# Writing the head sums of the attention output: four copies by ScalarE and one add in SBUF, in place of two copies and two adds out of PSUM

## The chip, the core and the metric

The kernel runs on one core of one Trainium2 chip. The metric is the device time of one execution in microseconds (us). The kernel before took 1492.64 us (median of 3 runs, 1490.17 to 1496.86). Engines are named as the profile names them: PE is TensorE (PEld its weight loads), ACT is ScalarE, DVE is VectorE, POOL is GpSimd, SP is the engine that issues the DMAs.

## The reference

One decoder layer over 1024 tokens of width 1024: stick-breaking attention with 16 heads of 64, a 4-head cross-attention into 256 memory tokens, one output projection, and a SwiGLU feed-forward part. What the change touches is the end of the stick-breaking attention, the product with the values:

```python
z = jnp.einsum('bhqd,bhkd->bhqk', qi, k).astype(jnp.float32) * SCALE
past = kpos[None, :] < tpos[:, None]
log_fail = jnp.where(past, jax.nn.log_sigmoid(-z), 0.0)
after = lax.cumsum(log_fail, axis=3, reverse=True) - log_fail
a = jnp.where(past, jnp.exp(jax.nn.log_sigmoid(z) + after), 0.0)
return jnp.einsum('bhqk,bhkd->bhqd', a.astype(v.dtype), v)
```

## The kernel before

Every matrix product is made in full precision out of rounded parts: each operand is split into a high part (fp32r, copied by ACT) and a low part (what is left, subtracted by DVE), and PE adds the products of the parts up in PSUM.

The attention runs over 8 head pairs, s = 0 to 7 (PAIRS). Pairs 0 to 5 run in a loop, so that addresses and semaphore counts there come out of registers; pairs 6 and 7 are written out. A pair has 12 units (UNITS: one query tile of 128 rows against up to 512 keys), and the units make four groups of two query tiles, which end at units 1, 3, 7 and 11 (GROUP_END). For a unit PE computes scores (line 310), ACT takes two sigmoids of them (fail, line 391, and succ, line 397), DVE scans fail (lines 478 and 483) and multiplies (line 491), PE transposes the product (line 320), ACT and DVE split the transposed weights (a_h, line 405, and a_l, line 504), and every second unit PE multiplies them with the values into o_ps, one bank of PSUM (line 336). Between these PE does filler: in pairs 0 to 6 the next pair's input projection (pe_part, line 282), in the last pair the output projection (pe_project, line 882). Each engine runs its own instructions strictly in the order written out in pe_step, act_step and dve_step, and the engines meet at semaphores.

The value product puts the high and the low half of v side by side as 128 stationary columns, so that o_ps holds, for head h, two halves of 64 partitions and 256 columns that must still be added: for h = 0 the heads' rows are 0 to 63 and the low part is in rows 64 to 127; for h = 1 it is the other way about. act_low_rows (lines 408 to 414) copies the two low quarters into pv_low, on the partitions of their heads. dve_heads (lines 507 to 517) then adds, in two instructions of 64 partitions, the high quarter out of PSUM and pv_low, into o_t (om_t for pairs 6 and 7). Semaphore s_pl counts the copies (low_part_copied), s_o the adds (heads_written). PE opens a new group in o_ps (start=True) only when s_o says that the group before has been added (line 331), and ACT overwrites pv_low only then (line 412).

For the groups ending at units 1, 3 and 7 both helpers are called one unit later, inside the pair: act_low_rows between act_high and act_fail, dve_heads after dve_weights. The group ending at unit 11 is handled at the pair's end: ACT does act_v (v_s high, line 384), then act_low_rows, then the next pair's act_fail for unit 2. DVE does it in dve_open (lines 519 to 526) of the next pair: two scans, dve_heads, dve_weights (line 491), dve_v (line 468). PE's first transposes of the next pair (line 320) wait for that dve_v, because they go to the same banks. In the last pair ACT and DVE also split the attention output and w_out for the output projection (lines 730 and 736), and POOL makes the low parts of w_out (line 736). The cross-attention has helpers of its own (lines 845 to 858), which the change leaves as they are.

Of the kernel before, what the change touches and what calls it, by code (L numbers as in the profile page):

```python
# [5 lines left out]
ALU = mybir.AluOpType  # L6
ACT = mybir.ActivationFunctionType
# [5 lines left out]
P = 128  # L13
BANK = 512
HD = 64
# [4 lines left out]
def trunk(nc, x, mem, attn_norm, mem_norm, w_mem_kv, xq_norm, xk_norm, w_out, ffn_norm, w_gate, w_up, w_down,  # L20
          sb_w_in, out):
    _, S, D = x.shape
# [3 lines left out]
    PAIRS = D // (2 * HD)  # L26
# [29 lines left out]
    with ExitStack() as ctx:  # L56
        cursor = [-(-nc.sbuf_base // 32) * 32]
        
        def at(name, shape, dt, off):
            return nc.alloc_sbuf_tensor_at(name, shape, dt, offset=off)  # L60
# [7 lines left out]
        def take(name, shape, dt=F32, columns=None):  # L68
            t = at(name, [shape[0], columns] if columns else shape, dt, cursor[0])
            cursor[0] += size(shape)  # L70
            return t

        def sem(name):
            return ctx.enter_context(nc.semaphore(name))
# [24 lines left out]
        o_t = take("o_t", [P, PAIRS * S])  # L99
# [25 lines left out]
        pv_low = take("pv_low", [P, 2 * P])  # L125
# [23 lines left out]
        om_t = at("om_t", [P, 2 * S], F32, mk_at)  # L149
# [29 lines left out]
        t_ps, j_ps, z_ps, o_ps = ps[:, 0:2], ps[:, 2:4], ps[:, 4:7], ps[:, 7]  # L179
# [26 lines left out]
        s_pl = sem("low_part_copied")  # L206
        s_o = sem("heads_written")
# [115 lines left out]
        def pe_values(pe, s, u, par):  # L323

            i, k0, w, _ = UNITS[u]
            w_first = UNITS[u - 1][2]
            opens = UNITS[u][3]
            pe.wait_ge(s_tl, 1 + TUSE * s + u + 1)
            if opens:
                g = (i - 1) // 2  # L330
                pe.wait_ge(s_o, 8 * s + 2 * g + 1)
            for h in range(2):
                for j in range(w // P):
                    q0 = 0 if j * P < w_first else P
                    for t, a in enumerate((a_h, a_l)):
                        mm = pe.matmul(o_ps[:, h * 2 * P + q0:(h + 1) * 2 * P],  # L336
                                       v_s[par][:, k0 // P + j, 2 * h:2 * h + 2, :].rearrange("p a d -> p (a d)"),
                                       a[:, h, j, q0:2 * P],
                                       start=(opens and h == 0 and j == 0 and t == 0), stop=False,
                                       skip_group_check=True)  # L340
            mm.then_inc(s_pv, 1)
# [66 lines left out]
        def act_low_rows(act, s, u):  # L408

            g = UNITS[u][0] // 2  # L410
            act.wait_ge(s_pv, 1 + NU // 2 * s + u // 2 + 1)
            act.wait_ge(s_o, 8 * s + 2 * g + 1)
            act.activation(pv_low[0:HD, :], o_ps[HD:P, 0:2 * P], ACT.Copy).then_inc(s_pl, 1)
            act.activation(pv_low[HD:P, :], o_ps[0:HD, 2 * P:4 * P], ACT.Copy).then_inc(s_pl, 1)

        def act_step(act, s, par, last=False):
            side = iter(SPLITS) if last else None
# [26 lines left out]
            if not last:  # L444
                act_v(act, 1 - par, 1 + TUSE * s + NU)
            act_low_rows(act, s, NU - 1)


# [57 lines left out]

        def dve_heads(dve, s, u):
            g = UNITS[u][0] // 2
            dve.wait_ge(s_pl, 8 * s + 2 * g + 2)
            for h in range(2):  # L510
                r = slice(HD * h, HD * h + HD)
                if isinstance(s, int) and s >= PAIRS - 2:
                    dst = om_t[r, (s - PAIRS + 2) * S + g * 2 * P:(s - PAIRS + 2) * S + (g + 1) * 2 * P]
                else:
                    dst = o_t[r, bass.ds(s * S + g * 2 * P, 2 * P)]
                dve.tensor_tensor(dst, o_ps[r, h * 2 * P:(h + 1) * 2 * P],
                                  pv_low[r, :], ALU.add).then_inc(s_o, 1)

        def dve_open(dve, s, par):

            dve_scan(dve, s, 1, 0)
            dve_scan(dve, s, 1, 1)
            if not (isinstance(s, int) and s == 0):
                dve_heads(dve, s - 1, NU - 1)
            dve_weights(dve, s, 1)
            dve_v(dve, par, TUSE * s)
# [129 lines left out]
        def turn_ps(g):  # L656

            return ps[:, (0, 1, 4, 5)[g % 4]] if g < XU0 else t_ps[:, g % 2]
# [46 lines left out]
        def operand(i):  # L705

            what, k, half = i
            if what == "w":
                return wo_raw[:, W_ORDER.index(i) % 4], wo_h[:, k], wo_l[:, k]
            c = slice(half * BANK, (half + 1) * BANK)  # L710
            if k in (PAIRS - 2, PAIRS - 1):
                src = om_t[:, (k - PAIRS + 2) * S + half * BANK:(k - PAIRS + 2) * S + (half + 1) * BANK]
            else:
                at_ = (k if k < PAIRS else k - 2) * S + half * BANK
                src = o_t[:, at_:at_ + BANK]
            return src, o_h[k][:, c], o_l[k][:, c]

        def act_split(act, i):
            what, k, half = i
            src, high, _ = operand(i)  # L720
            if i == SPLITS[0]:
                act.wait_ge(s_pj, W1)
            if what == "o" and k >= PAIRS - 2 and k < PAIRS:
                act.wait_ge(s_o, 8 * (k + 1) + 1)
            if what == "w":
                N = W_ORDER.index(i)
                act.wait_ge(s_wo[N % 4], 16 * (N // 4 + 1))
                if half:
                    act.wait_ge(s_op, NT if k < EARLY else 2 * NT)
            act.activation(high, src, ACT.Copy).then_inc(s_sh, 1)  # L730
# [7 lines left out]
        def wait_split(eng, i):  # L738

            e, n = LOW[i]  # L740
            eng.wait_ge(s_sl[e], n)
# [368 lines left out]
        def _(sp):  # L1110
# [27 lines left out]
            for N in range(2 * OC):  # L1138
                if N == 2:
                    sp.wait_ge(s_pj, W1 - 2)  # L1140
                if N == OC + 4:

                    sp.wait_ge(s_o, 8 * PAIRS + 1)
                    for t in range(NT):
                        sp.dma_start(x2[:, t, 0:BANK], xd[:, t, 0:BANK]).then_inc(s_x2l[0][t], 16)
                if N >= 4:
                    wait_split(sp, W_ORDER[N - 4])
                _, k, n = W_ORDER[N]
                sp.dma_start(wo_raw[:, N % 4], wod[:, k, n * BANK:(n + 1) * BANK]).then_inc(s_wo[N % 4], 16)
# [43 lines left out]
        def _(act):  # L1193
# [6 lines left out]
            for g in range(4):  # L1200
                act.wait_ge(s_xt, g + 1)
                for i in range(2):
                    last = act.activation(m_hh[:, 2 * g + i], turn_ps(g)[:, i * M:(i + 1) * M], ACT.Copy,
                                          scale=gains[:, 1, 2 * g + i:2 * g + i + 1])
                last.then_inc(s_xh, 1)
            for k in range(4):
                act_mem_w(act, k)
# [60 lines left out]
            for i in LATER + SECOND:  # L1268
                act_split(act, i)
# [265 lines left out]
```

## Time and profile before

| | |
|---|---|
| median of the runs | 1492.64 us |
| lowest and highest run | 1490.17, 1496.86 us |
| profiled execution | 1497.44 us, of which its span 1495.5 us |
| mean granted clock of TensorE | 0.976 |
| start, projections and cross-attention | 0 to 164 us |
| attention over 8 head pairs, with its last products | 164 to 683 us |
| output projection, feed-forward part | 683 to 1495 us |

The page's first part gives the busy time of each engine. Waits are told as "waiting engine and line <- releasing engine and line". A timeline row gives the start, the duration, engine, line and operation, and in brackets how long the engine had sat idle and who ended that. Instructions of an engine overlap by a little, so the distance between two starts, and not the duration, is what an instruction costs its queue.

### The profile page before, as it was taken

How to read it: one execution, taken by the hardware profiler on the slowest of the kernel's cores; microseconds unless marked ns; L12 is line 12 of the kernel's file. 1: busy time of each engine (PE TensorE's matmuls, PEld its weight loads, DVE VectorE, ACT ScalarE, POOL GpSimd, SP SyncE). 2: the span in 40 equal slices, each digit the busy share in tenths (PEclk: the TensorE clock that was granted, in tenths of full speed). 3: DMA queues.
4: the chain of work that ended last, by engine and by line, in shares of the span. 5: the costliest groups of instructions: out<-in, count | busy, mean ns of one | idle time of the engine just before them, and what ended most of it. 6: DMA issues, size and time to landing. Idle time of an engine off the chain costs nothing.

```text
span 1495.5 us, 19957 instructions
## 1 busy us (share of the span) xinstructions
PE 1433.4 (96%) x7212; PEld 1173.9 (79%) x7212; DVE 864.2 (58%) x1292; ACT 558.9 (37%) x947; POOL 30.0 (2%) x31
## 2 busy tenths in 40 slices
PE   6998899999999999699999999999999999999998
PEld 4776687787877878588887888888888888888887
DVE  5446798898988989795253353342525334252535
ACT  6444566565565655562242212121211212121110
POOL 0000000000000000213000000000000000000000
PEclk8997999999999999699999999999999999999999
DMA  6100100010000100104111211110211111021102
GB/s 211 43 14 15 29 22 22 24 33 28 21 21 22 35 27 30 40 18 149 35 57 39 72 60 40 45 56 28 70 42 56 42 42 56 28 71 43 57 14 113
DMA packets 92610, 69.91 MB, mean 47 GB/s; under 512 B 7312, under 2 KB 78992, under 8 KB 92560
## 3 DMA queue, kind: packets, MB, share of 16 engines
q1 hardware_dynamic: 92560, 69.24, 15.0%
q8 instruction: 32, 0.52, 0.2%
q14 instruction: 18, 0.15, 0.0%
HBM read 65.03 MB, written 4.19 MB: 46 GB/s over the span
## 4 chain that ended last, share of the span: by engine, by line
PE 89%; DVE 5%; ACT 2%; issue 2%; SPq 1%; DMA 0%; DVEq 0%; ACTq 0%
PE ps L989 32%; PE ps L1040 16%; PE ps L282 15%; PE ps L882 7%; PE ps L336 5%; PE ps L320 5%; PE ps L310 3%; PE ps L253 2%; PE ps L700 1%; PE ps L233 1%; PE ps L839 1%; DVE hl L682 1%; DVE succ L491 1%; DVE v_s L468 1%; PE ps L671 1%
## 5 line engine op out<-in xcount | busy, mean ns | idle before, releaser
L989 PE MATMUL ps<-f_h,gw_h 128*128 128x512 f32 x704 | 275.2, 391 | 1.9 <-DVE f_l L682 1.9
L989 PE MATMUL ps<-f_l,gw_h 128*128 128x512 f32 x704 | 274.6, 390 | 0.0
L989 PE MATMUL ps<-f_h,gw_l 128*128 128x512 f32 x704 | 274.5, 390 | 0.0
L1056 DVE TENSOR_TENSOR x<-ps,x 128x512 f32<-128x512 f32 x176 | 121.5, 691 | 80.7 <-PE ps L1040 77.5
L989 PEld LDWEIGHTS ps<-f_h,gw_h 128*128 128x128 f32 x704 | 132.5, 188 | 29.4 <-issue 2.1
L989 PEld LDWEIGHTS ps<-f_h,gw_l 128*128 128x128 f32 x704 | 132.6, 188 | 27.7
L989 PEld LDWEIGHTS ps<-f_l,gw_h 128*128 128x128 f32 x704 | 132.6, 188 | 27.4
L405 ACT ACTIVATE a_h<-ps 128x256 fp32r<-128x256 f32 (+2 forms) x96 | 78.0, 813 | 169.5 <-PE ps L320 169.4
L282 PE MATMUL ps<-hh,w_h 128*128 128x512 f32 x336 | 140.7, 419 | 0.0
L1040 PE MATMUL ps<-dw_h,gu_h 128*128 128x512 f32 x352 | 136.9, 389 | 0.0
L1040 PE MATMUL ps<-dw_l,gu_h 128*128 128x512 f32 x352 | 136.9, 389 | 0.0
L1040 PE MATMUL ps<-dw_h,gu_l 128*128 128x512 f32 x352 | 136.9, 389 | 0.0
L282 PE MATMUL ps<-hh,w_l 128*128 128x512 f32 x336 | 132.7, 395 | 0.0
L282 PE MATMUL ps<-hl,w_h 128*128 128x512 f32 x336 | 132.4, 394 | 0.0
L1014 DVE TENSOR_TENSOR prod<-ps,sig 128x512 f32<-128x512 f32 x44 | 30.4, 692 | 146.6 <-PE ps L989 133.4
L504 DVE TENSOR_TENSOR a_l<-ps,a_h 128x256 fp32r<-128x256 f32 (+2 forms) x96 | 91.6, 954 | 39.4 <-ACT a_h L405 38.6
L1021 ACT ACTIVATE gu_h<-prod 128x512 fp32r<-128x512 f32 x44 | 27.8, 632 | 213.6 <-DVE prod L1014 213.6
L478 DVE TENSOR_TENSOR_SCAN fail<-fail,own 128x129 f32<-128x129 f32 (+3 forms) x128 | 102.5, 828 | 1.5 <-ACT fail L391 1.3
L320 PE MATMUL ps<-ident,succ 128*128 128x128 f32 x576 | 83.0, 281 | 18.7 <-DVE a_l L504 8.1
L491 DVE TENSOR_TENSOR succ<-fail,succ 128x256 f32<-128x256 f32 (+2 forms) x96 | 93.6, 975 | 0.3
L966 ACT ACTIVATE gw_h<-f_raw 128x512 fp32r<-128x512 f32 x88 | 53.0, 625 | 104.1 <-DMA f_raw<-in_w_up 101.9
L320 PEld LDWEIGHTS ps<-ident,succ 128*128 128x128 f32 x576 | 65.4, 143 | 31.3 <-issue 10.4
(172 smaller groups left out, 2369.4 us busy)
## 6 DMA issues: line engine op xcount, KB each, us to landing
w_raw<-in_sb_w_in SPq DMA_DIRECT2D x52, 256.0 KB, 2.9
f_raw<-in_w_gate SPq DMA_DIRECT2D x44, 256.0 KB, 3.0
f_raw<-in_w_up SPq DMA_DIRECT2D x44, 256.0 KB, 2.9
f_raw<-in_w_down SPq DMA_DIRECT2D x44, 256.0 KB, 2.7
wo_raw<-in_w_out SPq DMA_DIRECT2D x20, 256.0 KB, 2.7
x_in<-in_x SPq DMA_DIRECT2D x8, 512.0 KB, 8.4
x<-in_x SPq DMA_DIRECT2D x16, 256.0 KB, 6.1
out<-x SPq DMA_DIRECT2D x8, 512.0 KB, 2.6
```

What stands on the lines that cost most here:

```text
L282: mm = pe.matmul(j_ps[:, 0], w[:, kc // 4, kc % 4], h[:, kc, half * BANK:(half + 1) * BANK], start=(kc == 0 and i == 0), stop=(kc == KC - ...
L320: mm = pe.transpose(t_ps[:, h, j * P:(j + 1) * P], succ[:, u % 2, h, j * P:(j + 1) * P], ident[:, :])
L336: mm = pe.matmul(o_ps[:, h * 2 * P + q0:(h + 1) * 2 * P], v_s[par][:, k0 // P + j, 2 * h:2 * h + 2, :].rearrange("p a d -> p (a d)"), a[:, ...
L405: act.activation(a_h[:, :, 0:w // P, col * P:(col + 1) * P], t_ps[:, :, 0:w].rearrange("p h (j q) -> p h j q", q=P), ACT.Copy).then_inc(s_ ...
L478: dve.tensor_tensor_scan(back, back, own[:, BANK - w:BANK + 1][:, ::-1], 0.0, ALU.mult, ALU.max).then_inc(s_scan, 1)
L491: done = dve.tensor_tensor(g, f[:, :, 1:w + 1], g, ALU.mult)
L504: dve.tensor_tensor(a_l[:, :, 0:w // P, c], t_ps[:, :, 0:w].rearrange("p h (j q) -> p h j q", q=P), a_h[:, :, 0:w // P, c].bitcast(F32), A ...
L882: mm = pe.matmul(out_bank(i), o[k][:, t * P:(t + 1) * P], w[:, k], start=(at_ == 0 and j == 0), stop=(at_ == len(order) - 1 and j == 2))
L966: act.activation(ffn_w(kind, par, j, True), (f_raw2 if extra_slot(r) else f_raw)[:, j % 2], ACT.Copy).then_inc(s_fh, 1)
L989: mm = pe.matmul(ps[:, 4 + 2 * fb + mat], w[:, fb, mat, k], f[half][:, k], start=(k == 0 and i == 0), stop=(k == KC - 1 and i == 2))
L1040: mm = pe.matmul(ps[:, (2, 3, 0, 1)[d % 4]], g[par][:, fb, t * P:(t + 1) * P], w[:, fb, n * BANK:(n + 1) * BANK], start=(fb == 0 and i == ...
L1056: dve.tensor_tensor(o, ps[:, (2, 3, 0, 1)[d % 4]], o, ALU.add).then_inc(s_x2, 1)
```

## The change

ACT now copies all four quarters out of o_ps: for each h first the low quarter into pv_low, then the high quarter straight into o_t (or om_t) at its place, given by a new helper heads_at. DVE adds pv_low to o_t in place, in SBUF, as one instruction over 128 partitions. So ACT has four copies for each group where it had two, and DVE one add where it had two. s_pl counts four for each group, s_o one. PE opens the next group when s_pl says that all four copies are made, no longer when DVE has added. DVE waits for all four copies; ACT still waits for the previous group's add before it overwrites pv_low. A count of one is added to s_pl at the kernel's start, by a copy of the memory tokens' part, as s_o has one from DVE, and the counts on s_o elsewhere (act_split, the SP queue) are adapted.

```diff
--- before.py
+++ after.py
@@ -328,7 +328,7 @@
             pe.wait_ge(s_tl, 1 + TUSE * s + u + 1)
             if opens:
                 g = (i - 1) // 2
-                pe.wait_ge(s_o, 8 * s + 2 * g + 1)
+                pe.wait_ge(s_pl, 16 * s + 4 * g + 1)
             for h in range(2):
                 for j in range(w // P):
                     q0 = 0 if j * P < w_first else P
@@ -409,9 +409,19 @@
 
             g = UNITS[u][0] // 2
             act.wait_ge(s_pv, 1 + NU // 2 * s + u // 2 + 1)
-            act.wait_ge(s_o, 8 * s + 2 * g + 1)
-            act.activation(pv_low[0:HD, :], o_ps[HD:P, 0:2 * P], ACT.Copy).then_inc(s_pl, 1)
-            act.activation(pv_low[HD:P, :], o_ps[0:HD, 2 * P:4 * P], ACT.Copy).then_inc(s_pl, 1)
+            act.wait_ge(s_o, 4 * s + g + 1)
+            for h in range(2):
+                r, other = slice(HD * h, HD * h + HD), slice(HD - HD * h, P - HD * h)
+                cols = slice(h * 2 * P, (h + 1) * 2 * P)
+                act.activation(pv_low[r, :], o_ps[other, cols], ACT.Copy).then_inc(s_pl, 1)
+                act.activation(heads_at(s, g, r), o_ps[r, cols], ACT.Copy).then_inc(s_pl, 1)
+
+        def heads_at(s, g, r):
+
+            if isinstance(s, int) and s >= PAIRS - 2:
+                at_ = (s - PAIRS + 2) * S + g * 2 * P
+                return om_t[r, at_:at_ + 2 * P]
+            return o_t[r, bass.ds(s * S + g * 2 * P, 2 * P)]
 
         def act_step(act, s, par, last=False):
             side = iter(SPLITS) if last else None
@@ -506,15 +516,9 @@
 
         def dve_heads(dve, s, u):
             g = UNITS[u][0] // 2
-            dve.wait_ge(s_pl, 8 * s + 2 * g + 2)
-            for h in range(2):
-                r = slice(HD * h, HD * h + HD)
-                if isinstance(s, int) and s >= PAIRS - 2:
-                    dst = om_t[r, (s - PAIRS + 2) * S + g * 2 * P:(s - PAIRS + 2) * S + (g + 1) * 2 * P]
-                else:
-                    dst = o_t[r, bass.ds(s * S + g * 2 * P, 2 * P)]
-                dve.tensor_tensor(dst, o_ps[r, h * 2 * P:(h + 1) * 2 * P],
-                                  pv_low[r, :], ALU.add).then_inc(s_o, 1)
+            dve.wait_ge(s_pl, 16 * s + 4 * g + 5)
+            both = heads_at(s, g, slice(0, P))
+            dve.tensor_tensor(both, both, pv_low[:, :], ALU.add).then_inc(s_o, 1)
 
         def dve_open(dve, s, par):
 
@@ -721,7 +725,7 @@
             if i == SPLITS[0]:
                 act.wait_ge(s_pj, W1)
             if what == "o" and k >= PAIRS - 2 and k < PAIRS:
-                act.wait_ge(s_o, 8 * (k + 1) + 1)
+                act.wait_ge(s_o, 4 * (k + 1) + 1)
             if what == "w":
                 N = W_ORDER.index(i)
                 act.wait_ge(s_wo[N % 4], 16 * (N // 4 + 1))
@@ -1140,7 +1144,7 @@
                     sp.wait_ge(s_pj, W1 - 2)
                 if N == OC + 4:
 
-                    sp.wait_ge(s_o, 8 * PAIRS + 1)
+                    sp.wait_ge(s_o, 4 * PAIRS + 1)
                     for t in range(NT):
                         sp.dma_start(x2[:, t, 0:BANK], xd[:, t, 0:BANK]).then_inc(s_x2l[0][t], 16)
                 if N >= 4:
@@ -1202,6 +1206,8 @@
                 for i in range(2):
                     last = act.activation(m_hh[:, 2 * g + i], turn_ps(g)[:, i * M:(i + 1) * M], ACT.Copy,
                                           scale=gains[:, 1, 2 * g + i:2 * g + i + 1])
+                    if g == 0 and i == 0:
+                        last.then_inc(s_pl, 1)
                 last.then_inc(s_xh, 1)
             for k in range(4):
                 act_mem_w(act, k)
```

## Rows read from the trace of the kernel before

**Rows 1.** the page: busy time, share of the span and instructions of each engine

```profile
PE 1433.4 (96%) x7212; PEld 1173.9 (79%) x7212; DVE 864.2 (58%) x1292; ACT 558.9 (37%) x947; POOL 30.0 (2%) x31
```

**Rows 2.** busy time of stretches of the attention, columns PE to POOL, granted clock, DMA

```profile
295.00:360.00 65.00, 62.49 (x384) 51.05 (x382) 56.12 (x74) 37.81 (x59) 0.00 (x0) 1.00 0.08 24
555.00:620.00 65.00, 56.33 (x347) 46.95 (x347) 53.38 (x70) 36.53 (x56) 2.75 (x2) 0.90 0.10 33
620.00:683.00 63.00, 56.16 (x313) 46.62 (x312) 54.45 (x63) 39.70 (x64) 11.39 (x8) 0.91 0.11 34
```

**Rows 3.** waits of 164 to 683 us: waiting engine, releaser, total, times, longest

```profile
DVE o_t L516 <- ACT pv_low L414: 22.3, 6, 3.7
PE ps L320 <- DVE a_l L504: 8.1, 8, 1.0
PE ps L320 <- DVE v_s L468: 6.7, 7, 3.5
```

**Rows 4.** instructions of line 516: duration ns min/median/max, first and last start

```profile
L516 DVEq FUSED_REGOPS  x48: 57/57/57, 180.0 to 543.7; - x48
L516 DVE TENSOR_TENSOR o_t<-ps,pv_low x48: 405/422/429, 181.7 to 544.1; 64x256 f32 x48
```

**Rows 5.** the first of the two copies into pv_low, same columns

```profile
L413 ACT ACTIVATE pv_low<-ps x32: 381/382/385, 179.2 to 680.4; 64x256 f32<-64x256 f32 x32
```

**Rows 6.** ScalarE in order of time, one pair's end: start, duration, instruction

```profile
291.85 1.03 ACT L384 ACTIVATE v_s<-ps 128x1024 fp32r<-128x1024 f32 x1 [2.16 <-PE ps L293]
292.90 0.38 ACT L413 ACTIVATE pv_low<-ps 64x256 f32<-64x256 f32 x1
293.31 0.38 ACT L414 ACTIVATE pv_low<-ps 64x256 f32<-64x256 f32 x1
293.71 0.81 ACT L391 ACTIVATE fail<-ps 128x768 f32<-128x768 f32 x1
```

**Rows 7.** VectorE in order of time, same stretch

```profile
288.52 0.41 DVE L491 TENSOR_TENSOR succ<-fail,succ 128x256 f32<-128x256 f32 x1
288.85 1.27 DVE L478 TENSOR_TENSOR_SCAN fail<-fail,own 128x257 f32<-128x257 f32 x2
293.83 0.88 DVE L516 TENSOR_TENSOR o_t<-ps,pv_low 64x256 f32 x2 [3.70 <-ACT pv_low L414]
294.74 0.69 DVE L491 TENSOR_TENSOR succ<-fail,succ 128x512 f32<-128x512 f32 x1
295.46 1.23 DVE L468 TENSOR_TENSOR v_s<-ps,v_s 128x1024 fp32r<-128x1024 f32 x1
```

**Rows 8.** TensorE in order of time, same stretch

```profile
296.74 0.44 PE L320 MATMUL ps<-ident,succ 128*128 128x128 f32 x2 [0.51 <-DVE v_s L468]
298.20 0.66 PE L320 MATMUL ps<-ident,succ 128*128 128x128 f32 x4 [1.02 <-DVE a_l L504]
```

**Rows 9.** ScalarE in order of time, a group inside a pair

```profile
317.80 0.60 ACT L405 ACTIVATE a_h<-ps 128x512 fp32r<-128x512 f32 x1 [1.21 <-PE ps L320]
```

**Rows 10.** all engines in order of time, last pair

```profile
632.68 0.38 ACT L414 ACTIVATE pv_low<-ps 64x256 f32<-64x256 f32 x1
634.90 0.63 ACT L730 ACTIVATE o_h<-o_t 128x512 fp32r<-128x512 f32 x1
635.57 0.69 DVE L736 TENSOR_TENSOR o_l<-o_t,o_h 128x512 fp32r<-128x512 f32 x1 [0.86 <-ACT o_h L730]
639.41 0.39 PE L336 MATMUL ps<-a_h,v_s 128*128 128x256 f32 x1 [0.65 <-DVE a_l L504]
```

**Rows 11.** GpSimd and VectorE in order of time, last pair

```profile
620.49 1.26 POOL L736 TENSOR_TENSOR wo_l<-wo_raw,wo_h 128x512 fp32r<-128x512 f32 x1 [6.16 <-ACT wo_h L730]
620.80 2.03 DVE L491 TENSOR_TENSOR succ<-fail,succ 128x1024 f32<-128x1024 f32 x1
```

**Rows 12.** busy time of shorter stretches, columns as in rows 2

```profile
116.00:120.00 4.00, 4.00 (x21) 3.42 (x20) 1.61 (x7) 0.67 (x2) 0.00 (x0) 0.61 0.01 4
355.00:360.00 5.00, 4.01 (x20) 2.56 (x16) 3.36 (x5) 2.16 (x6) 0.00 (x0) 1.00 0.00 0
```

## The prediction

> **What bounds the kernel now.** I read the page first: PE is busy for 96% of the span [rows 1]. Then the stretches: in a steady stretch of the attention PE is busy for 62.49 of 65 us, DVE for 56.12, ACT for 37.81 [rows 2]. So DVE is nearly full, but PE is fuller: all that a lighter DVE can give back in such a stretch is part of PE's 2.5 us of holes. Only where the last two pairs meet are the holes larger: 8.7 us from 555 to 620 and 6.8 us from 620 to 683, at a mean clock of 0.90 and 0.91 [rows 2].
>
> Third, the waits, to see who makes PE's holes. Seven times PE's transposes at a pair's start wait for DVE's v_s, 6.7 us in all, and eight times for a_l right behind, 8.1 us in all [rows 3]. No row of the waits has PE waiting for line 516, so the wait of pe_values that the change moves from s_o to s_pl is never late today. And DVE waits for ACT's copy at line 414: six times with 22.3 us in the loop [rows 3], that is 3.7 us at each pair's end.
>
> Fourth, the timelines of one pair's end, which put these waits into one chain. ACT copies v_s at 291.85, then the two low quarters at 292.90 and 293.31, and is past them at 293.71 [rows 6]. DVE has been idle for 3.70 us when it starts the adds at 293.83. Behind them stand the multiply of unit 1 (294.74) and the low part of v_s (295.46) [rows 7], and for that last one PE has been idle for 0.51 us when it goes on at 296.74 [rows 8]. This chain sets PE's time at seven pair ends. The second hole, 1.02 us [rows 8], is PE to ACT to DVE and back for unit 0: it keeps its length and moves with the first.
>
> **The change, part by part.** The sum is made on the profiled execution (1497.44 us, span 1495.5), as a difference, and carried to the median of 1492.64, which is 4.8 us (0.3%) lower.
>
> Two more copies of a quarter on ACT for each of 32 groups. One takes 0.382 us [rows 5]; from start to start, two cost 293.71 - 292.90 = 0.81 us [rows 6]. The new ones have the same shape and source and go to SBUF too, so I take 0.81 us for two, 26 us more for ACT in all. In the loop their destination comes out of a register, which no copy of this stage has today. Nearest is DVE's line 516, with a register operation of 57 ns for each [rows 4], and its instructions are no longer for it. I take nothing, since ACT's queue stands before instructions that are still running while it works addresses out; the other end is 57 ns and about as much again to issue it, 0.11 us for each copy, 0.23 for a group. Below nothing I exclude: nothing is taken from ACT.
>
> DVE's two adds become one. Today they hold the queue for 294.74 - 293.83 = 0.91 us [rows 7]. No add of 128 partitions by 256 columns out of SBUF into SBUF is there, but line 491 is a product of that very size, both inputs in SBUF: it takes 0.41 us and the next starts 0.33 us behind it [rows 7]. I take 0.33, a gain of 0.58 us for a group. The other end is an add as dear as the two together, a gain of zero; 0.44, if the next instruction can't overlap, lies between. Shorter than 0.33 I exclude, since the same number of columns takes that elsewhere.
>
> At a pair's end both lie in the chain. DVE waits for all four copies, so it starts 0.81 us later, and its queue is free 0.58 us sooner: the multiply, v_s and PE's transposes come 0.23 us later. Seven ends make 7 x 0.23 = 1.6 us. With the dear add it is 7 x 0.81 = 5.7 us; with the register operations on ACT 6 x 0.23 = 1.4 us come on top. Queued behind ACT's copies is the next pair's fail for unit 2, at 293.71; DVE scans it only behind v_s, which ends at 296.69 [rows 7], and the fail would be ready at 293.71 + 0.81 + 0.81 = 295.33, so this delay is covered by 1.4 us.
>
> Inside a pair three groups each put 0.81 us into ACT's queue ahead of fail, succ, a weight copy and the next a_h. ACT's idle time before that a_h is the cover: the tightest of a pair I found is 1.21 us, at 317.80 [rows 9], so 0.40 is left. If that cover were gone, a_h, a_l and then PE's value product would be late by what is missing. DVE gains 0.58 us there, but PE isn't waiting for it, so the gain becomes idle time of DVE. I cost all of this at nothing.
>
> The last pair is different, since ACT also makes the splits there and its queue is full. At unit 4 the copy at 632.68 is followed by fail, succ and the o_h of 634.90; DVE has been idle for 0.86 us when it takes the low part of that at 635.57, then scans, makes a_l, and PE has been idle for 0.65 us for it at 639.41 [rows 10]. Nothing in that chain has slack, and DVE's cheaper add lies before its own wait for o_h. So 0.81 us go to the path once. The other two groups of that pair stand before transposes that ACT waits for. Bounds: zero, if the 0.81 us are swallowed by a later wait for DVE, and 1.6 us, if a second group of that pair is as tight.
>
> Behind the last group the copies end 0.81 us later, the add some 0.2 us later, and with it SP's loads of x; PE is in projections that don't need them yet: nothing. PE's earlier leave to open a group is worth nothing, as no row has it waiting.
>
> The Trainium skill has a rule against this change ("SBUF — State Buffer", section Who interferes with whom): a DVE instruction with two SBUF inputs contends with a GpSimd instruction that reads SBUF, and one of them blocks for the whole of the other. Today's add has one input in PSUM, the new one has both in SBUF. In the last pair POOL makes wo_l at 620.49, and a DVE product that started at 620.80 took 2.03 us [rows 11], where 0.41 and 0.69 us for 256 and 512 columns [rows 7] give about 1.25 for its 1024: the trace agrees. By the rule each of the five adds that come after POOL's start could wait up to the 1.26 us of a POOL instruction, 6.3 us in all, and the sum would be 1501.4 us; today's adds would by it never wait. It is part of rival (d).
>
> Those five are the last group of pair 6 and the four of pair 7. The other 27 are free of this: POOL does nothing in the steady stretch (0.00 us) and 2.75 us from 555 to 620 [rows 2].
>
> Sum: 1.6 + 0.8 = 2.4 us, so 1492.6 + 2.4 = 1495.1 us.
>
> **The rivals.** (a) DVE's load counts after all. If DVE set the pace, a pair would gain 3 x 0.58 = 1.7 us and eight pairs 14 us: 1479 us. For it speaks DVE's 56 of 65 us [rows 2]; against it that PE's holes come from latency at a pair's start and not inside a pair, and that all holes of a steady stretch are 2.5 us. (b) The clock falls, slower than before. At a pair's end PE is busy for 4.01 of 5 us today and stays at 1.00 [rows 12], that is 2.4 GHz. The longer hole could let it fall to 1.2 GHz. The nearest price is the stretch from 116 to 120, where PE was busy throughout at a mean of 0.61 [rows 12]: 4 x 0.39 = 1.6 us of work lost. Six ends of the loop make 9.4 us: 1504.5. It decides from the point where the two holes, now 1.5 us together, lengthen enough; 0.23 us seems little, and a mean below 1.00 stands only beside holes of 7 to 9 us [rows 2]. (c) The add is as dear as the two it replaces, or the register operations stand in the path: 5.7 + 1.4 + 0.8 = 7.9 us, so 1500.5. Against it stands the product of the same size. (d) POOL and ACT's full queue in the last pair: two blocked adds and a second tight group, 2 x 1.26 + 0.8 more: 1498.4. (e) The change doesn't do what it says, for one if ACT's copies go slower side by side with PE's writes; the wait of 22.3 us [rows 3] would grow by more than 0.81 us an end. That ends like (c).
>
> **How the numbers follow.** A measurement of this kernel tells about 0.5% (7.5 us) from no change. The forecast has 0.74, (a) 0.06, (b) 0.06, (c) and (e) together 0.07, (d) 0.07. Of (a) two thirds would be over 7.5 us faster: 0.04. Slower by over 7.5 us are (b) and about half of (c) and (e): 0.10. The rest, 0.86, is within 0.5%. The range: below, the forecast without the last pair's 0.8 us and with the spread of the runs (2.5 us below the median) is 1491.8, and some 2 us for holes of the last two pairs that happen to close, 1490; above, (c) with a little of the spread, 1501.5.
>
> **What would show it.** In the changed kernel: four copies at 0.40 us from start to start; one add of about 0.41 us with the next instruction 0.33 us behind its start; DVE's idle time before it at a pair's end near 4.5 us where it was 3.70; PE's first hole of a pair near 0.75 us where it was 0.51; ACT's idle time before a_h of unit 5 near 0.4 us; DVE's busy time down by some 14 us and ACT's up by some 24 us, with a span almost unchanged. The prediction is wrong if PE's holes inside a pair shrink or grow, if the clock of a loop pair falls below 1.00, or if the add takes over 0.6 us.

## The result

The changed kernel took 1499.68 us (median of 20 runs, 1493.41 to 1501.25) against 1493.47 us for the kernel before (20 runs, 1488.17 to 1497.94). The ratio is 1.0032, with a 95% interval of 1.0021 to 1.0043: 4.8 us slower, between 3.1 and 6.4 (the medians lie 6.2 us apart, the means 5.1). That is beyond the measurement's uncertainty and within the 0.5% that the forecast counted as no change. Later runs of both kernels on another chip gave 1.0043 (1.0028 to 1.0058), 6.4 us. The forecast of 1495.1 us, 2.4 us slower, had the sign and half the size.

### The profile page after: what moved, and what is told of

Same layout as the page of the kernel before. It is cut to its first block, busy times and chain, and to the rows that moved or that the text cites. A ratio compares the mean times of both kernels' runs of the same rounds, so it can differ in the third digit from the quotient of the medians.

```text
span 1496.6 us, 20013 instructions
## 1 busy us (share of the span) xinstructions
PE 1432.8 (96%) x7212; PEld 1175.3 (79%) x7212; DVE 850.4 (57%) x1260; ACT 583.3 (39%) x1011; POOL 29.9 (2%) x31
## 4 chain that ended last, share of the span: by engine, by line
PE 88%; DVE 5%; ACT 3%; issue 2%; DMA 1%; SPq 1%; ACTq 0%; DVEq 0%
PE ps L993 31%; PE ps L1044 16%; PE ps L282 15%; PE ps L886 7%; PE ps L336 5%; PE ps L320 5%; PE ps L310 3%; PE ps L253 2%; PE ps L704 1%; PE ps L233 1%; PE ps L843 1%; DVE hl L686 1%; DVE v_s L478 1%; DMA mw_raw<-in_w_mem_kv 1%; PE ps L675 0%
```

## The profile of the changed kernel

The profiled execution took 1498.44 us, its span was 1496.6 us. Its first section, busy time and instructions of each engine, against [rows 1]:

```profile
PE 1432.8 (96%) x7212; PEld 1175.3 (79%) x7212; DVE 850.4 (57%) x1260; ACT 583.3 (39%) x1011; POOL 29.9 (2%) x31
```

DVE is 13.8 us lighter (864.2 to 850.4) and ACT 24.4 us heavier (558.9 to 583.3), as the change says. The spans differ by only 1.1 us because the start of the kernel, which the change leaves alone, happened to run 2.8 us faster in this execution; medians and stretches tell more than the two spans.

The instructions of the change, first those of o_t and pv_low (duration ns min/median/max), then ACT and DVE in order of time at one pair's end, against [rows 5], [rows 6] and [rows 7]:

```profile
L416 ACT ACTIVATE pv_low<-ps x64: 375/379/383, 176.4 to 681.9; 64x256 f32<-64x256 f32 x64
L521 DVE TENSOR_TENSOR o_t<-o_t,pv_low x24: 420/425/427, 178.9 to 542.7; 128x256 f32 x24
```

```profile
351.21 1.03 ACT L384 ACTIVATE v_s<-ps 128x1024 fp32r<-128x1024 f32 x1 [2.16 <-PE ps L293]
352.26 0.38 ACT L416 ACTIVATE pv_low<-ps 64x256 f32<-64x256 f32 x1
352.67 0.38 ACT L417 ACTIVATE o_t<-ps 64x256 f32 x1
353.07 0.38 ACT L416 ACTIVATE pv_low<-ps 64x256 f32<-64x256 f32 x1
353.47 0.38 ACT L417 ACTIVATE o_t<-ps 64x256 f32 x1
353.87 0.81 ACT L391 ACTIVATE fail<-ps 128x768 f32<-128x768 f32 x1
```

```profile
353.99 0.42 DVE L521 TENSOR_TENSOR o_t<-o_t,pv_low 128x256 f32 x1 [4.54 <-ACT o_t L417]
354.33 0.69 DVE L501 TENSOR_TENSOR succ<-fail,succ 128x512 f32<-128x512 f32 x1
354.94 1.22 DVE L478 TENSOR_TENSOR v_s<-ps,v_s 128x1024 fp32r<-128x1024 f32 x1
```

Four copies stand 0.40 us apart, the register operations of two of them cost nothing that can be seen, and ACT is past them 1.61 us after the first began, where two took 0.81. The add takes 0.42 us and the multiply starts 0.34 us behind it. New is the next distance: v_s starts 0.61 us behind the multiply, where it was 0.72 in [rows 7]. PE in order of time, against [rows 8]:

```profile
356.21 0.44 PE L320 MATMUL ps<-ident,succ 128*128 128x128 f32 x2 [0.65 <-DVE v_s L478]
357.65 0.66 PE L320 MATMUL ps<-ident,succ 128*128 128x128 f32 x4 [1.01 <-DVE a_l L514]
```

The first hole of a pair is 0.65 us here, where this pair's was 0.54 in the trace before; the second is unchanged. In the six pair ends that open pairs 1 to 6, the first hole grew from 0.51 to 0.59 us to 0.61 to 0.71 us: 0.10 to 0.12 us each.

So far this is a change of 0.1 us. What the forecast had only as an unlikely rival is in the stretches behind two of the pair ends (columns as in [rows 2]: busy time of PE, PEld, DVE, ACT and POOL, granted clock, DMA):

```profile
354.00:358.00 4.00, 2.34 (x12) 1.49 (x11) 3.58 (x6) 1.93 (x4) 0.00 (x0) 1.00 0.00 0
358.00:362.00 4.00, 4.00 (x25) 3.48 (x24) 4.00 (x6) 3.38 (x5) 0.00 (x0) 1.00 0.22 65
416.00:420.00 4.00, 2.42 (x11) 1.47 (x9) 3.18 (x6) 1.89 (x4) 0.00 (x0) 1.00 0.00 0
420.00:424.00 4.00, 3.94 (x13) 3.23 (x14) 4.00 (x6) 3.19 (x5) 0.00 (x0) 0.57 0.23 66
424.00:428.00 4.00, 4.00 (x34) 3.44 (x33) 2.58 (x4) 1.84 (x4) 0.00 (x0) 1.00 0.00 0
546.00:550.00 4.00, 3.61 (x12) 2.96 (x13) 4.00 (x6) 3.44 (x5) 0.00 (x0) 0.59 0.22 66
```

Behind the hole that ends at 356.21 the clock stays at 1.00. Behind those that end at 418.60 and 544.96 it falls: 4 us at a mean of 0.57 are 4 x 0.43 x 2 = 3.4 us at 1.2 GHz, and PE is busy in nearly all of them. The pairs that follow these two ends last 63.92 and 63.88 us from first hole to first hole, those without a fall 62.37 to 62.45. A fall here means a stretch of the loop at 1.2 GHz behind a pair's end. (Behind the much longer hole at the start of pair 7, 3.49 us before and 3.59 us now, both kernels run 24 us at 1.2 GHz; that does not tell them apart.)

The last pair, all engines in order of time, against [rows 10]:

```profile
633.50 0.38 ACT L417 ACTIVATE om_t<-ps 64x256 f32<-64x256 f32 x1
...
635.73 0.63 ACT L734 ACTIVATE o_h<-o_t 128x512 fp32r<-128x512 f32 x1
...
636.39 0.69 DVE L740 TENSOR_TENSOR o_l<-o_t,o_h 128x512 fp32r<-128x512 f32 x1 [2.06 <-ACT o_h L734]
...
640.10 0.39 PE L336 MATMUL ps<-a_h,v_s 128*128 128x256 f32 x1 [1.30 <-DVE a_l L514]
```

Each step of the chain that the prediction wrote out is there 0.8 us later after the copies, and PE's hole went from 0.65 to 1.30 us.

Putting the two traces on one scale (a pair starts here where PE's first hole ends; in us):

| from, to | before | changed |
|---|---|---|
| start of pair 1 to start of pair 7 | 234.06 to 608.85: 374.79 | 231.39 to 608.84: 377.45 |
| of it falls of the clock | none | 2 |
| start of pair 7 to the projection's last hole | 608.85 to 687.03: 78.18 | 608.84 to 688.08: 79.24 |
| from there to the end | 808.47 | 808.52 |

## The experiments

The theory after the result: the changed kernel makes the chain at a pair's end only 0.1 us longer, but with it the clock now falls at some pair ends, 1.5 us each, where with the shorter holes before it fell at none; the last pair adds about 1 us. The rivals: ACT's greater load costs inside the pairs, or DVE's lighter load matters and something else eats the gain. The runs were made on several chips; each ratio is to the kernel before on the same chip, with its 95% interval, and a count of falls is that of one trace. "First hole" is PE's wait for v_s at a pair's start, "second hole" the wait for a_l behind it.

### ScalarE's part alone

dve_heads is that of the kernel before, over four copies, and PE waits for its adds again (the edit against the changed kernel; ... marks what is left out):

```diff
-            both = heads_at(s, g, slice(0, P))
-            dve.tensor_tensor(both, both, pv_low[:, :], ALU.add).then_inc(s_o, 1)
+            for h in range(2):
...
+                dve.tensor_tensor(dst, o_ps[r, h * 2 * P:(h + 1) * 2 * P],
+                                  pv_low[r, :], ALU.add).then_inc(s_o, 1)
```

> The ScalarE part of the change alone: four copies for each group as in the changed kernel, but VectorE still makes its two adds out of PSUM (over what ScalarE wrote into o_t), and TensorE waits for these adds as before. Theory (pair-end chain and clock): nothing is taken from the chain, so TensorE's first hole of a pair goes from 0.51 us to about 1.3 us (+0.81), 7 x 0.8 = 5.7 us, and the last pair adds 0.8; the longer holes also let TensorE's clock fall at most of the six pair ends of the loop, 1.5 us each: 7 to 15 us slower than before, ratio 1.005 to 1.010. Rival (it is ScalarE's load inside the pairs that costs): TensorE shows new holes inside pairs, and the first hole of a pair explains less than half of the loss. Rival (VectorE's load counts): as VectorE gains nothing here, the loss is over 10 us without any fall of the clock.

Measured: 1.0109 (1.0091 to 1.0126), 16 us slower. The waits of PE at the starts of pairs 1 and 2, and the clock behind the latter:

```profile
233.40 0.44 PE L320 MATMUL ps<-ident,succ 128*128 128x128 f32 x2 [1.34 <-DVE v_s L478]
```

```profile
298.18 0.44 PE L320 MATMUL ps<-ident,succ 128*128 128x128 f32 x2 [1.31 <-DVE v_s L478]
```

```profile
300.00:304.00 4.00, 4.00 (x13) 3.15 (x12) 3.88 (x5) 2.76 (x4) 0.00 (x0) 0.57 0.23 64
```

The first hole is 1.31 to 1.39 us, the 0.81 more that the two copies cost, and the clock falls behind five of the six ends. 7 x 0.8 for the holes, 5 x 1.5 for the clock and 0.8 us in the last pair are 13.9 us; a further 1.0 us is one more hole of that pair (3.40 us where it was 2.37). These 14.9 us are within the interval of the loss (13.6 to 18.8 us), which is somewhat above the 7 to 15 us expected; it is at the pairs' ends.

### VectorE's part alone

The kernel leaves the high half of the product out of its output; the counts on s_pl are adapted to two copies:

```diff
-                act.activation(heads_at(s, g, r), o_ps[r, cols], ACT.Copy).then_inc(s_pl, 1)
...
-            dve.tensor_tensor(both, both, pv_low[:, :], ALU.add).then_inc(s_o, 1)
+            dve.tensor_tensor(both, pv_low[:, :], pv_low[:, :], ALU.add).then_inc(s_o, 1)
```

> The VectorE part of the change alone: ScalarE makes its two copies as before, VectorE makes one add of 128 partitions in SBUF (pv_low to itself), and TensorE waits for the copies. The high half of the value product is left out of the output. Theory (pair-end chain and clock): the chain is 0.70 us shorter (in the changed kernel the two starts behind the add come 0.58 and 0.12 us sooner), the hole of 0.51 us closes, 6 x 0.51 + 0.7 in the last pair = 3.8 us, and no fall of the clock at a pair's end: 3 to 5 us faster than before, ratio 0.997 to 0.998. Rival (VectorE's load counts): a pair gains 1.7 us, 14 us in all, ratio 0.991. Rival (ScalarE's load inside pairs): same gain as the first, so it is told apart by the run with four copies.

Measured: 0.9969 (0.9955 to 0.9983), 4.6 us faster. The first hole is gone from the loop, no pair end there has a fall, and a pair lasts 61.6 us. The 14 us of "VectorE's load counts" are excluded. So the two parts are worth +16 and -5 us by themselves and +5 us together. They do not add up: the chain is 0.69 us shorter here, but a first hole of 0.51 to 0.59 us can't give back more than its length, and the clock fell at no end with two copies and one add, at five with four copies and two adds, and at two and four with both parts.

### The changed kernel with the add behind multiply and v_s

```diff
-            if not (isinstance(s, int) and s == 0):
-                dve_heads(dve, s - 1, NU - 1)
             dve_weights(dve, s, 1)
             dve_v(dve, par, TUSE * s)
+            if not (isinstance(s, int) and s == 0):
+                dve_heads(dve, s - 1, NU - 1)
```

> The changed kernel with VectorE's add of a pair's last group moved behind the multiply of unit 1 and the low part of v_s, so that the four copies of ScalarE are no longer in the chain that TensorE waits for at a pair's start. ScalarE's load inside the pairs is as in the changed kernel. Theory (pair-end chain and clock): the first hole of a pair closes (0.62 us six times, and over 2 us of the 3.59 us before the last pair), and the clock stays at 1.00 at the ends of the loop's pairs: about 6 us for the holes and 3 to 4 us for the clock less than the changed kernel, ratio to before 0.996 to 0.998. Rival (ScalarE's load inside the pairs): the loss stays, ratio above 1.001.

Measured: 0.9957 (0.9943 to 0.9972), 6.4 us faster than before. Against the changed kernel that is some 11 us (the ratios of both to the kernel before differ by 0.0075), with all of the change's load on ACT still there. The waits of PE in the whole attention (waiting engine, releaser, total, times, longest):

```profile
PE ps L320 <- DVE a_l L514: 8.6, 8, 1.5
...
PE ps L320 <- DVE v_s L478: 1.0, 1, 1.0
```

The first hole is left once, before the last pair, 1.03 us where it was 3.59, and the clock stays at 1.00 in the loop. That settles ACT's load: it costs nothing inside the pairs of the loop.

### The kernel before with the same move

> The kernel before with the same move of VectorE's adds behind the multiply and v_s. Theory: the hole of 0.51 us closes at each pair's start and 2 to 3 us of the 3.49 us before the last pair go: 5 to 6 us faster than before, ratio 0.996 to 0.997, and within 0.1% of the changed kernel with the same move, since then the change touches no chain except that of the last pair (0.7 us against it). Rival (ScalarE's load): this kernel is faster than the changed one with the move by the whole 0.3%.

Measured: 0.9956 (0.9940 to 0.9972), the same as the changed kernel with the move. With its adds out of that chain, the change is worth nothing measurable either way. The traces show two small effects that work against each other: from the start of pair 1 to that of pair 7 this kernel takes 368.55 us and the changed one with the move 367.39 us, 1.2 us less, and in the last pair the changed one has the longer hole (1.31 us where this one has 0.65).

### Lengthening the hole of the kernel before

Two doses, in VectorE's queue between the adds and the multiply of unit 1:

```diff
+            for _ in range(1):
+                dve.tensor_copy(g_cross[:, 0:1], g_cross[:, 1:2])
             dve_weights(dve, s, 1)
```

> The kernel before, with one tiny VectorE copy (128x1) put between the adds and the multiply of unit 1 at each pair's start: it lengthens the chain, and TensorE's first hole of a pair, by 0.08 to 0.2 us and changes nothing else (ScalarE's two copies and VectorE's two adds stay). Theory (clock): this is the changed kernel's lengthening without its change, so the clock falls at some of the six pair ends of the loop, not the same number in each run, 1.5 us each: 2 to 6 us slower than before, of which 0.6 to 1.4 us are the holes themselves; ratio 1.001 to 1.004. Rival (the changed kernel lost its 3 to 4 us elsewhere, by ScalarE's load or in the last pair): only the holes, 1 us, ratio 1.000 to 1.001.

Measured: 1.0010 (0.9997 to 1.0022), not distinguishable from no change. The tiny copy lengthened the first hole by only 0.05 us (0.56 to 0.65), less than the smallest dose expected (0.08), and the trace has one fall. By itself this run decides nothing.

```diff
+            for k in range(2):
+                dve.tensor_tensor(spare[:, k], ident[:, 0:96], ident[:, 0:96], ALU.add)
             dve_weights(dve, s, 1)
```

> The same place with two VectorE adds of 128x96 between adds and multiply: the hole is lengthened by 0.3 to 0.5 us. Theory (clock): the fall comes at nearly every pair end of the loop: 7 x 0.4 = 2.8 us of holes and 6 x 1.5 = 9 us of clock, 9 to 12 us slower, ratio 1.006 to 1.008. Rival (no clock): 2 to 3.5 us, ratio 1.0015 to 1.0025.

Measured: 1.0060 (1.0043 to 1.0077), 9.0 us slower, for 0.33 us more at each start, 2.3 us in all.

```profile
293.51 0.44 PE L321 MATMUL ps<-ident,succ 128*128 128x128 f32 x2 [0.84 <-DVE v_s L469]
294.96 0.98 PE L321 MATMUL ps<-ident,succ 128*128 128x128 f32 x4 [1.01 <-DVE a_l L505]
```

```profile
295.00:299.00 4.00, 4.00 (x13) 3.34 (x14) 4.00 (x5) 3.09 (x5) 0.00 (x0) 0.57 0.24 66
486.00:490.00 4.00, 3.73 (x12) 3.11 (x13) 3.88 (x6) 3.40 (x5) 0.00 (x0) 0.57 0.22 66
```

Five of the six ends have a fall: 2.3 + 5 x 1.5 = 9.8 us. "No clock" expected 3.5 us at most and is excluded.

### Less idle time at the pair's start, without a shorter chain

Three matmuls of the projection of unit 1 go ahead of that unit's transposes (pe_part is cut in two for it):

```diff
+                if u == 1 and not last:
+                    pe_part(pe, s + 1, 1 - par, 0, 4, 0)
                 if u:
                     pe_transposes(pe, s, u)
```

> The changed kernel with three matmuls (0.69 us) of the projection of unit 1 moved ahead of unit 1's transposes, into TensorE's second hole of a pair. The first hole keeps its 0.62 us, ScalarE and VectorE do what they do in the changed kernel. Theory (clock and holes): second hole 1.02 to about 0.33 us, 7 x 0.69 = 4.8 us, and with half the idle time at a pair's end no fall of the clock there: 7 to 9 us faster than the changed kernel, ratio to before 0.997 to 0.999. Rival (the clock falls with the length of the first hole alone): it stays, and the ratio is 0.999 to 1.000.

Measured: 1.0012 (0.9999 to 1.0024), 3.0 us faster than the changed kernel by the two ratios, and not the 7 to 9 us expected. PE's timeline shows why:

```profile
354.00 0.44 PE L320 MATMUL ps<-ident,succ 128*128 128x128 f32 x2 [0.65 <-DVE v_s L480]
354.60 0.50 PE L282 MATMUL ps<-hh,w_h 128*128 128x512 f32 x1 [0.16 <-DVE w_l L466]
...
364.12 1.09 PE L320 MATMUL ps<-ident,succ 128*128 128x128 f32 x8 [0.53 <-DVE succ L503]
```

```profile
354.00:358.00 4.00, 3.84 (x18) 2.87 (x19) 3.57 (x6) 3.44 (x6) 0.00 (x0) 1.00 0.23 66
416.00:420.00 4.00, 3.45 (x17) 2.51 (x18) 3.56 (x6) 3.04 (x6) 0.00 (x0) 1.00 0.23 66
```

The second hole shrank to the 0.16 us in front of line 282, but 0.5 us came back at 364.12 as a wait for DVE's multiply of unit 3 (line 503), which has not become any earlier: up to pair 6 a pair still lasts 62.36 to 62.49 us. A pair with the same work and the same length has the same time to spare, only spread out, and the clock stays at 1.00 at all six ends of this trace. From pair 1 to pair 7 it takes 374.30 us, as much as the changed kernel's 377.45 less its two falls of 1.5 us. So in the traces the gain is that of the clock alone. Here the theory's count of the holes was wrong, and its part on the clock held. The two intervals (this one and 1.0021 to 1.0043) still overlap by 0.0003, so the times by themselves leave it open; the traces carry the verdict.

> The kernel before with three matmuls of the projection of unit 1 ahead of unit 1's transposes, as in the changed kernel with that move, where it took the falls of the clock away but not the idle time (0.5 us came back as a wait for VectorE's product of unit 3). Theory: the kernel before has few falls to lose, so the same move gains less here than the 0.2% (3 us) it gained in the changed kernel: ratio 0.9985 to 1.000. Rival (the move is worth 3 us for another reason than the clock): the same 0.2%, ratio 0.998.

The same move in the kernel before: 0.9999 (0.9984 to 1.0014). It had no falls to lose, and nothing was gained: its trace takes 374.76 us from pair 1 to pair 7, where the kernel before took 374.79.

### Both moves in the changed kernel

> The changed kernel with both moves, VectorE's adds behind multiply and v_s, and three matmuls ahead of unit 1's transposes. Theory: the first hole is closed and the second is 0.33 us; to the 0.9957 of the late add alone come 7 x 0.69 = 4.8 us: ratio to before 0.992 to 0.993. Rival (VectorE or ScalarE sets the pace once the pair's start is full): the gain of the second move is under 2 us, ratio above 0.9945.

Measured: 0.9962 (0.9947 to 0.9977), no better than the late add alone. The rival held: once the pair's start is filled, DVE's multiply of unit 3 is late by the same amount, here too.

```profile
355.98 0.66 PE L320 MATMUL ps<-ident,succ 128*128 128x128 f32 x4 [0.31 <-DVE a_l L516]
...
364.66 1.09 PE L320 MATMUL ps<-ident,succ 128*128 128x128 f32 x8 [0.55 <-DVE succ L503]
```

### Both kernels once more

> The kernel before, unchanged, for a second trace of it and the granted clock of its runs. Theory (clock): with holes of 0.51 and 1.02 us the clock falls at few of the six pair ends of the loop, at most one or two in this trace; ratio 0.999 to 1.001.

> The changed kernel, unchanged, beside it on the same chip. Theory (clock): its trace shows the clock at 1.2 GHz for some 3 us behind two to six of the pair ends of the loop, 1.5 us each, and the mean granted clock of its runs is lower than that of the kernel before by 0.002 to 0.005; ratio 1.002 to 1.004. Rival (no clock): equal clocks within 0.001, and pair periods of equal length behind every end.

Measured: 1.0000 (0.9984 to 1.0017) and 1.0043 (1.0028 to 1.0058). The second trace of the kernel before has again no fall at a pair end of the loop, that of the changed kernel has four. One stretch of each, behind the start of pair 4:

```profile
421.00:425.00 4.00, 3.92 (x22) 3.37 (x23) 4.00 (x6) 3.63 (x6) 0.00 (x0) 1.00 0.24 66
```

```profile
424.00:428.00 4.00, 4.00 (x13) 3.14 (x12) 3.23 (x4) 2.10 (x3) 0.00 (x0) 0.57 0.13 40
```

From the start of pair 1 to that of pair 7 the second traces take 374.71 us (before) and 380.45 us (changed); with two falls the changed kernel took 377.45. So a fall costs (380.45 - 377.45) / 2 = 1.5 us. The mean granted clock of the runs points the same way for executions without a trace: 0.9755 over the changed kernel's first 20 runs and 0.9749 over seven later ones, against 0.9794 to 0.9800 for three sets of the kernel before, 71 runs in all. A fall of 3.4 us to half the clock lowers the mean of a run by 3.4 x 0.5 / 1495 = 0.0011, so by this estimate an execution of the changed kernel has some four falls more, if nothing else moved its mean.

Falls of the clock behind the six pair ends of the loop, by what PE's holes are there:

| kernel | first hole, us | second hole, us | falls |
|---|---|---|---|
| before, two traces | 0.50 to 0.59 | 1.02 | 0 and 0 |
| before, matmuls moved | 0.50 to 0.60 | 0.16; 0.37 to 0.55 some 10 us behind the first hole | 0 |
| before, lengthened by 0.05 | 0.56 to 0.65 | 1.02 | 1 |
| changed, two traces | 0.61 to 0.71 | 1.02 | 2 and 4 |
| before, lengthened by 0.33 | 0.84 to 0.93 | 1.02 | 5 |
| four copies, two adds | 1.31 to 1.39 | 1.02 | 5 |
| changed, matmuls moved | 0.62 to 0.71 | 0.16; 0.36 to 0.55 some 10 us behind the first hole | 0 |
| one add, two copies | none | 1.02 | 0 |
| late add, both kernels | none | 1.02 | 0 and 0 |
| changed, both moves | none | 0.31 to 0.33; 0.36 to 0.56 behind it, as above | 0 |

## Why the prediction was right, and where it was not

**What bounds the kernel.** Right: PE, with holes made by the chain at a pair's end. With the adds taken out of that chain, either kernel is some 6.5 us faster than the kernel before.

**The copies.** Right: 0.81 us for two more, nothing for the register operations, DVE's idle time before the add 4.54 us where about 4.5 was forecast. In the run with four copies and two adds the first hole grew by 0.80 us.

**The add.** The distance to the next instruction is 0.34 us against 0.33 forecast. But the gain was put at 0.58 us and is 0.69 (from the add's start to that of v_s 0.94 us where it was 1.63): v_s too starts 0.11 us sooner behind the multiply (0.61 us against 0.72). I had compared one distance and should have followed the queue to the instruction that PE waits for. The Trainium skill ("VectorE: DVE Perf Modes", section Two Vector instructions with no wait between them) has a rule that fits: an instruction waits for the earlier ones to end if its input starts in another group of 32 partitions than the last input from the same memory. Before, the last PSUM input in front of v_s was that of the add of partitions 64 to 127; now it is one that starts at partition 0. The traces agree, with these two distances and two more. In pair 0 of the changed kernel no add stands in front, and the last input from PSUM was that of the cross-attention's second add, on partitions 64 to 127; there v_s starts 0.72 us behind the multiply, although the kernel is the changed one:

```profile
161.36 0.87 DVE L861 TENSOR_TENSOR o_t<-ps,pv_low 64x256 f32<-64x256 f32 x2 [2.12 <-ACT pv_low L854]
...
166.05 0.69 DVE L501 TENSOR_TENSOR succ<-fail,succ 128x512 f32<-128x512 f32 x1
166.77 1.23 DVE L478 TENSOR_TENSOR v_s<-ps,v_s 128x1024 fp32r<-128x1024 f32 x1
```

And in the kernel with two adds of 128 partitions in SBUF between the adds out of PSUM and the multiply (the lengthening by 0.33 us) it is 0.72 us too, so the kind of instruction right in front isn't what counts. No run here changed the partition alone.

**The pair's end.** 0.23 us were forecast, 0.10 to 0.12 came: 0.8 us in all at seven ends and not 1.6.

**Inside a pair.** ACT's cover held, as forecast: its idle time before a_h of unit 5 is 0.43 us, where 0.40 was worked out.

```profile
314.87 0.60 ACT L405 ACTIVATE a_h<-ps 128x512 fp32r<-128x512 f32 x1 [0.43 <-PE ps L320]
```

DVE's gain was put at nothing and was not quite that. Before, PE came 0.16 to 0.35 us later to the value product of unit 9 in every second pair than it does now (in pair 1 the trace names the wait, 0.19 us for a_l); with the lighter DVE this is gone. So the loop without its falls is 377.45 - 2 x 1.5 = 374.45 us, 0.3 us shorter than before, although its first holes are longer by 0.7 us in all: the lighter DVE gives back about 1 us. The two kernels with the late add show the same (367.39 us against 368.55).

**The last pair.** 0.8 us forecast, 0.7 measured at PE (1.30 us of hole less 0.65 and the few hundredths around it). The end behind the last group was put at nothing and cost 0.4 us: the last add ends later against the projection, SP's loads of x with it, and so POOL starts its work on x only 0.24 us ahead of DVE's splits of line 740 (686.09 and 686.33), where it had been 0.63 us ahead. The first split ends some 0.55 us behind POOL's first instruction in both traces, so more of that instruction now lies within it; the pair of splits takes 3.30 us where it took 2.92, and PE's hole there is 0.88 us where it was 0.50.

```profile
686.09 2.98 POOL L906 TENSOR_TENSOR x<-part,x 128x512 f32<-128x512 f32 x2 [7.61 <-DMA x<-in_x]
...
686.33 3.30 DVE L740 TENSOR_TENSOR o_l<-om_t,o_h 128x512 fp32r<-128x512 f32 x2 [3.21 <-ACT o_h L734]
...
688.08 0.47 PE L886 MATMUL ps<-wo_h,o_h 128*128 128x512 f32 x1 [0.88 <-DVE o_l L740]
```

I had looked at whether PE needs the loads of x, not at what POOL would do to DVE once they land.

**Rival (b), the clock, is the step that failed.** The prediction names as signs of its being wrong that the clock of a loop pair falls below 1.00 and that holes inside a pair shrink or grow; both came, the second by tenths of a microsecond. Without the falls the terms are 0.1 (first pair) - 0.3 + 1.1 = about 0.9 us. The measured 4.8 us leave 3.9 us, which is 2.6 falls of 1.5 us (1.5 to 3.7 over the interval of the ratio); two and four were seen. I had priced a fall rightly (1.6 us), placed it rightly (the six ends of the loop), and then treated it as one case that either comes at all six ends or at none, with a chance of 0.06, because 0.23 us "seems little". It took 0.1 us, and it comes at some ends and not at others. The sum should have held a term of six times a chance times 1.5 us. That the measured time lies inside the range is in part luck: with a fall at all six ends it would have been 0.9 + 9 = some 10 us slower, 1502.5 us, and outside.

The argument that a mean below 1.00 stands only beside holes of 7 to 9 us doesn't hold for the trace of the kernel before. There the clock falls at the start of the attention behind holes of 0.79 and 1.10 us:

```profile
164.62 0.44 PE L310 MATMUL ps<-k_h,q_h 64*128 64x384 f32 x2 [0.79 <-ACT succ L397]
...
166.52 0.49 PE L310 MATMUL ps<-k_h,q_h 64*128 64x512 f32 x2 [1.10 <-ACT succ L397]
```

```profile
167.00:170.30 3.30, 3.30 (x12) 2.17 (x9) 2.80 (x4) 0.17 (x1) 0.00 (x0) 0.50 0.00 0
```

These two holes are 1.9 us together, not far from a pair end's 1.5 us. They were there to be read before the result.

**Rival (a)**, DVE's load: excluded by the run with one add (4.6 us and not 14), but for the fractions of a microsecond in unit 9. **Rival (c)**, a dear add: excluded, 0.42 us. **Rival (d)**, POOL blocking the new add: none of the 32 adds took over 0.43 us. But none ran during an instruction of POOL either, but for 0.03 us at 633.91. So the two-input rule of the Trainium skill ("SBUF — State Buffer", section Who interferes with whom) was not put to the test at the adds. What it describes is seen at other instructions, in both kernels: the product at 620.78 takes 2.03 us, as the one of [rows 11] did before, and the splits of the row at 686.33 are drawn out. **Rival (e)**, slower copies: excluded, they stand 0.40 us apart as before.

## What to carry to other kernels

Work that is moved off a busy engine is worth only what it shortens of a chain that another engine waits for, and its new place may lie in the same chain: here 0.69 us were taken from DVE and 0.81 us put on ACT one step ahead of it. Look first whether the step must stand in that chain at all: with the adds moved behind what TensorE waits for, either kernel was some 6.5 us faster than the kernel before, where trading instructions between the engines cost 5 us.

Where TensorE is nearly full, look at all its holes that lie close together before adding to one of them, and look through the whole trace for falls behind holes of that size; here a tenth of a microsecond more cost fifteen times its length through the clock, at some pair ends and not in every run alike.

A filler moved into a hole helps the clock, but it helps the time only if the next wait isn't late for the same reason.

## What the runs showed of the hardware

Two holes of 0.50 to 0.59 and 1.02 us with 0.44 us of transposes between them left TensorE at 2.4 GHz in all twelve cases of two traces; 0.61 to 0.71 and 1.02 us let it fall to 1.2 GHz in six of twelve, 0.84 to 0.93 and 1.02 in five of six. With the second hole filled by three matmuls and up to 0.55 us of idle time some 10 us behind the first instead, there was no fall in six. In the loop a fall lasted 3.4 us each time and cost 1.5 us. Nothing in the program says which pair ends are hit: the same kernel had two in one execution and four in another. The runs of the changed kernel go from 1493 to 1501 us at mean clocks of 0.981 down to 0.973. Not all of that spread is of the pair ends: runs of the kernel before, which has no fall there in either trace, go from 1488 to 1498 us, and its two traces differ in the first 171 us, with 44 and 34 us at 1.2 GHz.

ScalarE copies that change the starting partition of input or output from one to the next, as all four of a group do, stand 0.40 us apart at 0.38 us each, as the two copies did before; the changed kernel's fail and succ behind each other, on all partitions, overlap (311.98 with 1.03 us, then 312.90):

```profile
311.17 0.38 ACT L416 ACTIVATE pv_low<-ps 64x256 f32<-64x256 f32 x1
311.57 0.38 ACT L417 ACTIVATE o_t<-ps 64x256 f32 x1
311.98 1.03 ACT L391 ACTIVATE fail<-ps 128x1024 f32<-128x1024 f32 x1
312.90 1.02 ACT L397 ACTIVATE succ<-ps 128x1024 f32<-128x1024 f32 x1
```

What makes the difference wasn't tried.
